# A float32 decoder trunk on one core: the activations' buffer in chunks of 1056 bytes, every other buffer on multiples of 1024

## The reference: what is computed

```
for l in range(2):
    x = x + hybrid_mixer(rms_norm(x), w_in, ..., w_out)      # conv group and mLSTM group
    x = x + memory_cross_attention(rms_norm(x), rms_norm(mem), w_xq, w_xk, w_xv, w_xo)
    x = x + peer_ffn(rms_norm(x), w_pq, sub_keys, u_experts, v_experts)
return rms_norm(x)
```

## Time and profile before

| what | us |
|---|---|
| median of 2 runs | 2074.69 (2074.56 to 2074.82) |
| span of the profiled execution | 2075.4 |
| PE busy | 2051.7 (99%), 11544 matmuls |
| PE weight loads busy | 1757.1 |
| DVE busy | 1644.9 (79%) |
| ACT busy | 1192.1 (57%) |
| POOL busy | 338.7 (16%) |
| DMA | 435.54 MB, mean 210 GB/s |

### The profile page before, as it was taken

The page is one execution under the profiler, slowest core; times in us unless marked ns, Lnnn a source line. Parts: engine busy times, 40 slices in busy tenths (PEclk is TensorE's granted clock), DMA queues, the critical chain, the costliest instruction groups (busy, mean ns, idle before and its releaser), DMA issues.

```text
span 2075.4 us, 38360 instructions
## 1 busy us (share of the span) xinstructions
PE 2051.7 (99%) x11544; PEld 1757.1 (85%) x11544; DVE 1644.9 (79%) x3041; ACT 1192.1 (57%) x1901; POOL 338.7 (16%) x342
## 2 busy tenths in 40 slices
PE   8999999999999999999999999999999999999998
PEld 6888888888888888888888888888888898888886
DVE  7786769999998676776788858799999986676676
ACT  6555556667666555555565545566666665555553
POOL 4010110000000433333340101000000003333331
PEclk9999999999999999999999999999999999999999
DMA  6455467776566877777653554577666568777773
GB/s 221 146 163 162 162 203 231 235 234 212 192 196 200 282 242 241 241 241 241 208 187 122 185 180 160 197 229 234 217 215 193 196 211 280 242 243 241 241 241 127
DMA packets 174249, 435.54 MB, mean 210 GB/s; under 512 B 19504, under 2 KB 85040, under 8 KB 173136
## 3 DMA queue, kind: packets, MB, share of 16 engines
q1 hardware_dynamic: 173520, 430.06, 63.8%
q0 software_dynamic: 640, 4.32, 0.6%
HBM read 397.60 MB, written 36.70 MB: 209 GB/s over the span
## 4 chain that ended last, share of the span: by engine, by line
PE 93%; DVE 3%; ACT 1%; DMA 1%; issue 1%; SPq 0%; POOL 0%; DVEq 0%; ACTq 0%
PE ps L1315 33%; PE ps L1696 31%; PE ps L1316 17%; PE ps L1671 3%; PE ps L1587 2%; PE ps L1309 2%; DVE w_lo L833 1%; DMA raw<-slabs 1%; PE ps L1718 1%; PE ps L1612 1%; PE ps L1646 1%; PE ps L1569 1%; DMA h_park<-h_out 0%; ACT w_hi L710 0%; PE ps L1485 0%
## 5 line engine op out<-in xcount | busy, mean ns | idle before, releaser
L833 DVE TENSOR_TENSOR w_lo<-raw,w_hi 128x1024 fp32r<-128x1024 f32 x674 | 836.8, 1242 | 274.3 <-ACT w_hi L778 198.2
L1315 PE MATMUL ps<-act,w_hi 128*128 128x512 f32 x2784 | 988.8, 399 | 0.0
L1316 PE MATMUL ps<-act,w_lo 128*128 128x256 f32 x2784 | 778.2, 280 | 0.0
L1315 PEld LDWEIGHTS ps<-act,w_hi 128*128 128x128 f32 x2784 | 522.9, 188 | 120.4 <-issue 3.3
L1696 PE MATMUL ps<-w_hi,act 128*128 128x512 f32 x1936 | 597.2, 390 | 0.6 <-DVE act L1236 0.6
L1316 PEld LDWEIGHTS ps<-act,w_lo 128*128 128x128 f32 x2784 | 525.7, 189 | 0.1
L778 ACT ACTIVATE w_hi<-raw 128x1024 fp32r<-128x1024 f32 x248 | 263.1, 1061 | 321.9 <-PE ps L1696 311.4
L1696 PEld LDWEIGHTS ps<-w_hi,act 128*128 128x128 f32 x1936 | 363.6, 188 | 76.9 <-DVE act L1236 1.4
L1696 PE MATMUL ps<-w_lo,act 128*128 128x512 f32 x968 | 377.1, 390 | 0.0
L509 POOL TENSOR_TENSOR h_in<-h_in,gate 128x256 f32<-128x256 f32 x250 | 235.3, 942 | 446.4 <-DMA h_in<-h_park 446.2
L710 ACT ACTIVATE w_hi<-raw 128x1024 fp32r<-128x1024 f32 x248 | 261.1, 1053 | 0.0
(11 more groups left out here) (261 smaller groups left out, 1830.4 us busy)
## 6 DMA issues: line engine op xcount, KB each, us to landing
raw<-slabs SPq DMA_DIRECT2D x680, 512.0 KB, 4.2
h_park<-h_out SPq DMA_DIRECT2D x256, 128.0 KB, 2.1
h_in<-h_park SPq DMA_DIRECT2D x250, 128.0 KB, 3.9
memT<-mem POOLq DMA_DIRECT2D x2, 1024.0 KB, 6.2
skT<-sub_keys POOLq DMA_DIRECT2D x2, 1024.0 KB, 7.1
x_park<-xT SPq DMA_DIRECT2D x2, 1024.0 KB, 5.7
xT<-x_park SPq DMA_DIRECT2D x2, 1024.0 KB, 7.7
xT<-x SPq DMA_DIRECT2D x4, 256.0 KB, 6.3
```

The lines of the kernel that those rows point to most:

```text
L833: nc.vector.tensor_tensor(w_lo[:, j].rearrange("p k c -> p (k c)"), raw[:, j, :], w_hi[:, j].rearrange("p k c -> p (k c)").bitcast(FP32), ...
L1315: nc.tensor.matmul(ps[:, j, :], w_hi[:, j, k, :], a[:, :, k, :], start=(k == 0), stop=False)
L1316: return nc.tensor.matmul(ps[:, j, hi * T:hi * T + T], w_lo[:, j, k, :], a[:, hi, k, :], start=False, stop=(k == KB - 1))
```

## The change

Four things are moved, and no instruction is added, removed or reordered:

- `base` is rounded up to a multiple of 1024, so `raw`, `w_hi`, `w_lo`, `xT` and the start of `act_2` begin at multiples of 1024.
- The chunks of `act_2` are 264 floats (1056 bytes) apart and 256 of them are used. Chunk `k` of the high part begins at 32 `k` past a multiple of 1024, chunk `k` of the low part at 256 + 32 `k`. The two parts lie 8448 bytes apart instead of 8192.
- `y_nat` and `h_in` follow the chunks inside `act_2`.
- `gated_at` is rounded up to a multiple of 1024, so `mem_2`, `pre_2` and `gate` have the same place within 1024 bytes as the slabs' buffers. The small constants between move by whole multiples of 32 bytes.

```diff
--- before.py
+++ after.py
@@ -31,6 +31,8 @@
 ds = bass.ds
 
 P = 128
+LINE = 1024
+CHUNK_GAP = 8
 D = 1024
 KB = D // P
 T = 256
@@ -148,7 +150,7 @@
 def trunk(nc, x, mem, slabs, params, sub_keys, out):
     ctx = ExitStack()
     with ctx:
-        base = (nc.sbuf_base + 63) // 64 * 64
+        base = (nc.sbuf_base + LINE - 1) // LINE * LINE
         limit = nc.sbuf_usable_end
         ctx.enter_context(nc.sbuf_tensor("arena", [P, (limit - base - 64) // 4], FP32))
         top = [base]
@@ -172,11 +174,11 @@
         x_at = top[0]
         xT = sb("xT", [P, KB, T])
         act_at = top[0]
-        act_2 = sb("act_2", [P, 2, KB, T], F32R)
+        act_2 = sb("act_2", [P, 2, KB, T + CHUNK_GAP], F32R)[:, :, :, 0:T]
         act_hi, act_lo = act_2[:, 0], act_2[:, 1]
 
-        y_nat = [at(f"y_nat{b}", act_at + (2 * b + 1) * RING * T * 4, [P, 2, 512]) for b in range(TB)]
-        h_in = at("h_in", act_at + RING * T * 4, [P, RING, T])
+        y_nat = [at(f"y_nat{b}", act_at + (2 * b + 1) * RING * (T + CHUNK_GAP) * 4, [P, 2, 512]) for b in range(TB)]
+        h_in = at("h_in", act_at + RING * (T + CHUNK_GAP) * 4, [P, RING, T])
 
         hot_cols = [at(f"hot_col{i}", x_at + i * 1024, [P, 2, P, 2], FP16) for i in range(HOTS)]
         hot_rows_2 = [at(f"hot_row{i}", x_at + 2048 + i * 2048, [P, 2, PARTS, P, 2], FP16) for i in range(HOTS)]
@@ -201,6 +203,7 @@
         pick_at = at("pick_at", top[0], [P, 2, T // 2, 2], FP16)
         g_parts = at("g_parts", top[0] + 2 * T * 2, [P, T // 2, PARTS, 2], FP16)
         top[0] += (2 + PARTS) * T * 2
+        top[0] = (top[0] + LINE - 1) // LINE * LINE
         gated_at = top[0]
         gate = sb("gate", [P, NKEYS, T])
```

## The result

The changed kernel takes 2093.78 us (median of 2 runs, 2092.65 to 2094.91) against 2074.69: a ratio of 1.0086, 95% interval 1.0069 to 1.0103. It is slower by 0.9%, where a gain of 0.3% was forecast. The profiled execution has a span of 2093.2 us, 17.8 more than before.

What follows compares the result with a forecast made beforehand. PE was taken as the bound, by the time between matmul starts. Gains of 2.2 and 4.9 us, 7.1 in all, from the profiled 2075.4 gave 2068.3, the median 0.7 lower: 2068 us, range 2020 to 2093.

Steps and rivals of the forecast that it cites:

- The reading of the bound: Whole kernel: PE busy 99%, held up by no engine or DMA; 13 to 20 ns lost per fp32r matmul.
- the cover: Expert loop: DVE busy 165.10 of 175 us, so a pair can shorten by 6% before DVE sets the pace.
- `mem` and `pre` to the slabs' place: Memory values and wide pairs on `mem` and `pre`: 1.3 us and 0.9 us, together 2.2 us of gain.
- `act_2` streaming: Lines 1315, 1316, 1309, 2784 pairs: the 1056-byte step keeps the fast value for all, a gain of 4.9 us.
- the slow pattern: Layer 1's expert loop, 353.3 ns a pair: lasts because chunks share one place within 1024; the step should break it.
- `act_2` stationary: Lines 1696 and 1718, 3072 matmuls: no change taken; bounds 34 us less and 21 us more.
- the memory values' 233.6: Tiles 64 bytes past the streams' place: 233.6 ns a matmul against the `v` stage's 226.9, pointing up by 6.7.
- line 1440's 113 ns: Weight tiles 32 bytes apart, 24 matmuls of 256 columns: 113 ns against 120.0, pointing down by 7.0.
- the `v` stage pays as the memory values do: Rival, line 1696 slots 1 to 3: 6.7 ns x 3072 = 20.6 us more, 2089 us; chance 0.22.
- The rule: Skill's independent PE read ports for streams and weight loads: places cannot matter, time stays 2074.7; weighed against the trace.

Runs made afterwards that it cites:

- Experiment 1: Changed kernel with the chunks of `act_2` 1024 bytes apart again, only the alignment kept: 2073.79 us, ratio 0.9993 to the kernel before.
- experiment 5: Changed kernel with the `v` stage alone using its operand in chunks 1024 apart, 1056 kept elsewhere: 2078.77 us, ratio 1.0013 to the kernel before.
- experiment 6: Changed kernel, chunks 1024 apart, `act_2` 32 bytes past where it streams, `v` stage's own view at place 0: 2071.11 us, ratio 0.9977 to the kernel before.

## Why the prediction was wrong

- **The reading of the bound was right**: PE by the spacing of its matmuls. PE's largest waits are as before, and DVE had the cover in the expert loops.
- **`mem` and `pre` to the slabs' place: right in sign, too large in all.** The memory values went from 233.6 to 227.6 ns (forecast 226.9), 192 x 6.0 ns or 1.15 us of the 1.3. The wide pairs on them gained nothing. The 349.0 of `pre` was one window of layer 0; over the whole trace before, start to start inside a slab, `pre` had 351.6 and `mem` 349.0 ns, and after it is 351.6 and 350.0, with both the low and the high price in places. So the 0.9 us rested on a window, and at place 0 these pairs have two prices like those on `act_2`. Experiment 1 as a whole is 0.07% faster, where alignment alone was worth 2.2 us (0.1%) in the sum.
- **`act_2` streaming: this step failed too, in sign.** The step does break the slow pattern that one loop had. But it breaks the fast one too. The text took "the fast value of now for all", 346.7; measured is a mean of 350.7. Instead of a gain of 4.9 us there is a loss of 3 to 4: some 15 of the 17.8 us are the `v` stage (5.0 ns for 3072 matmuls), and the other 2 to 3 are net of the gain of 1.15 on the memory values. A pattern that repeats over hundreds of pairs is no sign that only the slow one depends on the constant place.
- **`act_2` stationary: the step that failed.** The text put one row against the other, the memory values' 233.6 against line 1440's 113 ns, "one points up, one down", and took no change. Measured is +5.0 ns for 3072 matmuls, 15 us, and experiment 5 gives it back. Line 1440 loads 8 columns and streams 256, and was the weaker row. Its 113 ns came from times rounded to 0.1 us; the starts in the trace give 115.1 in layer 0 and 116.6 in layer 1, so it pointed down by 3 to 5 ns, not by 7.0. And with weights of 128 columns the triples of line 1309 became only 1.3% cheaper (11.37 against 11.52 us). The row with the same instruction and a displaced tile was the memory values', and it held in three slots of four with nearly its price, 233.3 ns against 233.6.
- **The rival named the outcome**: "the `v` stage pays as the memory values do", 2089, with 0.22. Its mechanism came true and its number only by luck: it named slots 1 to 3 as the place but charged all 3072 matmuls, 20.6 us, where three quarters of them make 15.4. What it had too much there was more than made up by the gains of 7.1 us that did not come and the loss of the streaming pairs. The range ended at 2093, a hair below the median of 2093.78.
- **The rule weighed against the trace.** From the Trainium skill's "PE and ACT never wait on anyone" (SBUF — State Buffer, Who interferes with whom) the prediction drew that places cannot matter. For plain float32 that holds here, but the rows that show it are not those of line 1569, whose two operands lie in one area and keep their relative place. The transposes of `y_nat` show it: its tiles had the place of `ident` within 256 bytes before, are 128 off after, and eight still take 1.03 us, 109 ns from start to start:

```profile
1031.49 1.03 PE L1391 MATMUL ps<-ident,y_nat 128*128 128x128 f32 x8
```
```profile
1040.60 1.03 PE L1394 MATMUL ps<-ident,y_nat 128*128 128x128 f32 x8
```

  For fp32r places do matter: moving only the stationary tile by 32 bytes costs 6.6 ns of 226.9. Whether that is a wait at the two read ports that the section calls independent, or something else inside PE, no run shows.

What stays open is the mechanism below the law. The runs show that the relative place modulo 256 bytes sets the price of a long run in the `v` stage, and that the plain float32 transposes pay nothing for 128 bytes; none took the weight load away or looked below the spacing.

## What to carry to other kernels

Where one instruction on the bounding engine appears with two prices in one trace, find what differs and treat the dearer row as the price of becoming like it; don't net it against a row of another shape. With fp32r products like the `v` stage's (512 columns that stream against tiles of 128), keep stationary tiles at the same place within 256 bytes as what streams against them; for the wide pairs here 32 bytes past was the better place, so try both. Check the spacing of matmuls, not their durations, after any change of the allocation. A stagger that helps one use of a buffer can cost in another: give each use its own view, as experiment 6 does.

## What the runs showed of the hardware that was not expected

- A displacement of 32, 64, 128 or 224 bytes of the stationary tile costs 5.4 to 6.6 ns of 226.9 per 512-column fp32r matmul; 256 costs nothing.
- Streaming from `act_2` 32 bytes past the weights makes the triples of 256 columns cheaper (11.20 against 11.51 us for 96) and holds the wide pair at its low price; displaced by 224 the pair costs 353.1 ns.
- DVE's subtraction into `act_lo` (line 1236) went from 745 to 863 ns on average with the change, and from 748 to 829 with a displacement of 32, while its other large instruction, `w_lo`, stayed at 1242. With the `v` stage's tiles back on multiples of 1024 (experiment 5) it is 747 again. It cost next to nothing here, 1.2 us of waiting on PE in all against 0.6 before. It is not what makes PE slower: the memory values paid for their 64 bytes before the change, in a stage where line 1236 does not run. Its own cause was not looked for:

```profile
L1236 DVE TENSOR_TENSOR act<-h_in,act 128x256 fp32r<-128x256 f32 x250 | 186.3, 745 | 6.3 <-ACT act L766 6.3
```
```profile
L1239 DVE TENSOR_TENSOR act<-h_in,act 128x256 fp32r<-128x256 f32 x250 | 215.8, 863 | 6.2 <-ACT act L769 6.2
```
